# Moving the merge of the dilated branches from VectorE to GpSimd in the blocks of a hybrid attention encoder

## The reference

```python
for window, d in DIL_BRANCHES:              # (128,1), (512,4), (2048,16)
    o, lse = banded_attention(to_sub(q)[:, :, None], to_sub(k), to_sub(v), ...)
w = jax.nn.softmax(jnp.stack(lses), axis=0)
o = jnp.einsum("nbhs,nbhsd->bhsd", w, jnp.stack(outs).astype(jnp.float32))
...
y = jnp.concatenate([rms_norm(merge_heads(oa), ga),
                     rms_norm(merge_heads(ob), gb),
                     rms_norm(merge_heads(oc), gc)], axis=-1)
```

## Time and profile before

| | |
|---|---|
| median of three runs | 2626.75 us (2621.09 to 2628.8) |
| the profiled execution | 2627.53 us, its span 2625.8 us |
| mean granted TensorE clock | 0.977 |
| TensorE busy | 2497.4 us, 95% |
| VectorE busy | 1704.0 us, 65% |
| ScalarE busy | 1061.5 us, 40% |
| GpSimd busy | 515.4 us, 20% |

### The profile page before, as it was taken

The page is one execution under the profiler, slowest core; times in us unless marked ns, Lnnn a source line. Parts: engine busy times, 40 slices in busy tenths (PEclk is TensorE's granted clock), DMA queues, the critical chain, the costliest instruction groups (busy, mean ns, idle before and its releaser), DMA issues. The chain is left out here.

```text
span 2625.8 us, 36088 instructions
## 1 busy us (share of the span) xinstructions
PE 2497.4 (95%) x12576; PEld 2069.1 (79%) x12576; DVE 1704.0 (65%) x3236; ACT 1061.5 (40%) x2072; POOL 515.4 (20%) x414
## 2 busy tenths in 40 slices
PE   6999899989899999999989999999898999999997
PEld 5987787768688888888878878877686888888886
DVE  4288767852755555689844986677447555556896
ACT  3333655543522222344343336555444322223442
POOL 1000210000454544200000003100004444542000
PEclk9999999979999999999989999999799999999999
DMA  5311520022222222541232115100331222226213
GB/s 180 93 48 40 117 70 20 20 98 85 72 81 86 83 71 59 179 151 59 70 127 83 48 37 132 50 20 20 107 108 49 89 80 89 65 65 246 92 52 117
DMA packets 229540, 220.35 MB, mean 84 GB/s; under 512 B 48880, under 2 KB 190576, under 8 KB 229360
## 3 DMA queue, kind: packets, MB, share of 16 engines
q1 hardware_dynamic: 229360, 218.07, 26.3%
HBM read 169.96 MB, written 48.06 MB: 83 GB/s over the span
## 5 line engine op out<-in xcount | busy, mean ns | idle before, releaser
L2131 PE MATMUL psum<-OPH_t,WH 128*128 128x512 f32 x704 | 276.5, 393 | 15.9 <-DVE WL L1643 7.6
L2131 PE MATMUL psum<-OPL_t,WH 128*128 128x512 f32 x704 | 275.4, 391 | 0.0
L2131 PE MATMUL psum<-OPH_t,WL 128*128 128x512 f32 x704 | 275.1, 391 | 0.0
L1643 DVE TENSOR_TENSOR WL<-RAW,WH 128x512 fp32r<-128x512 f32 x132 | 161.8, 1226 | 162.8 <-ACT WH L1149 162.8
L2164 PE MATMUL psum<-ABH 128*128 128x512 f32 x616 | 240.1, 390 | 1.1 <-DVE X L1729 1.1
L2166 PE MATMUL psum<-ABH,ABL 128*128 128x512 f32 x616 | 239.7, 389 | 0.0
L2165 PE MATMUL psum<-ABL,ABH 128*128 128x512 f32 x616 | 239.7, 389 | 0.0
L1016 ACT ACTIVATE T<-T,G 128x192 f32<-128x192 f32 (+3 forms) x352 | 166.0, 472 | 144.4 <-DVE G L1394 141.9
L2131 PE MATMUL psum<-OPH_b,WH 128*128 128x512 f32 x528 | 205.6, 389 | 0.0
L2131 PE MATMUL psum<-OPH_b,WL 128*128 128x512 f32 x528 | 205.4, 389 | 0.0
L2131 PE MATMUL psum<-OPL_b,WH 128*128 128x512 f32 x528 | 205.4, 389 | 0.0
(11 more groups left out here) (214 smaller groups left out, 5417.7 us busy)
## 6 DMA issues: line engine op xcount, KB each, us to landing
RAW<-in_w_gu SPq DMA_DIRECT2D x176, 256.0 KB, 3.8
WDS<-in_w_down SPq DMA_DIRECT2D x88, 256.0 KB, 2.6
UR<-in_w_in SPq DMA_DIRECT2D x56, 256.0 KB, 3.2
g_mid<-GRES SPq DMA_DIRECT2D x28, 512.0 KB, 2.6
WDK<-in_w_down SPq DMA_DIRECT2D x44, 256.0 KB, 6.1
x_res<-X SPq DMA_DIRECT2D x2, 4096.0 KB, 13.5
PR<-in_w_out SPq DMA_DIRECT2D x32, 256.0 KB, 4.5
X<-x_res SPq DMA_DIRECT2D x2, 4096.0 KB, 13.0
```

Of the source, the lines that this page charges most:

```text
L1643: v.tensor_tensor(WL[SLOT[i, j]][:, :, :], w_source(i, j), WH[SLOT[i, j]][:, :, :].bitcast(F32), ALU.subtract).then_inc(w_lo, 1)
L2131: last = t.matmul(dst[:, :], w[SLOT[i, j]][:, k, :], h[o][:, k, :], start=(i in (1, 5, 6) and k == 0 and part == 0), stop=(i in (2, 3, 4) ...
```

## The change

The five operations of the merge (three multiplications by the factors, two additions) are issued by GpSimd, in a function `merge(b)` between the power operation of family b and that of family a, for every block but the last. Each raises a new semaphore `merge_s`; the additions wait for the operation that they build on. VectorE waits for all five in step 9 and takes the reciprocal there. What follows for C moves one step back: YC to step 10, `c_merged` and the squares to 11, the mean to 12, the scaling to 13. A's reciprocal, product, squares and mean and B's scaling keep their steps, A's scaling stays in 9. The tail is a function of its own, `tail_finish`, with the operations and the order of before, on VectorE.

```diff
-            LINKS_OWN, LINKS_LATE = 5, 15
+            LINKS_OWN, LINKS_LATE = 5, 10
...
-                def late_finish(b, s, tail=False):
-                    if s in (0, 1, 2, 3, 4, 5, 6, 7, 8, 9, 10, 11):
+                def late_finish(b, s):
+                    if s < 13:
                         dve.wait_ge(dve_seq, links())
...
                     elif s == 3:
-                        if tail:
-                            dve.wait_ge(tail_squares, 1)
                         mean(1, 384)
+                    elif s == 4:
+                        dve.wait_ge(grp_s, C_GROUPS + 3 * b + 3)
+                        link(v.reciprocal(den[:, 1, 0:4].unsqueeze(2), ga[:, :, HD:V1]))
+                    elif s == 5:
+                        link(v.tensor_tensor(YA.rearrange("p (h d) -> p h d", d=HD), ga[:, :, 0:HD],
+                                             spread(den[:, 1, 0:4], 4), ALU.mult))
+                        scale_y("b", b)
+                    elif s == 6:
+                        squares(0, YA, 256)
+                    elif s == 7:
+                        mean(0, 256)
+                    elif s == 9:
+                        dve.wait_ge(merge_s, 5 * b + 5)
+                        link(v.reciprocal(den[:, 2, :].unsqueeze(2), gc0[:, :, HD:V1]))
+                        scale_y("a", b)
+                    elif s == 10:
+                        link(v.tensor_tensor(YC.rearrange("p (h d) -> p h d", d=HD), gc0[:, :, 0:HD],
+                                             spread(den[:, 2, :], 6), ALU.mult))
+                    elif s == 11:
+                        dve.sem_inc(c_merged, 1)
+                        squares(2, YC, 384)
+                    elif s == 12:
+                        mean(2, 384)
+                    elif s == 13:
+                        scale_y("c", b)
...
+                def merge(b):
+                    pool.wait_ge(c_fac, b + 1)
+                    for i in range(3):
+                        g.tensor_tensor(GC[:, i, 0:6 * V1].rearrange("p (h d) -> p h d", d=V1),
+                                        GC[:, i, 0:6 * V1].rearrange("p (h d) -> p h d", d=V1),
+                                        fac_c[:, i, :].unsqueeze(2).broadcast_to([P, 6, V1]), ALU.mult).then_inc(merge_s, 1)
+                    for i in (1, 2):
+                        pool.wait_ge(merge_s, 5 * b + 2 + i)
+                        g.tensor_tensor(GC[:, 0, 0:6 * V1], GC[:, 0, 0:6 * V1], GC[:, i, 0:6 * V1],
+                                        ALU.add).then_inc(merge_s, 1)
+
                 for b in range(MT):
-                    for fam in (1, 0, 2):
-                        mean_powers(fam, b)
+                    mean_powers(1, b)
+                    if b < MT - 1:
+                        merge(b)
+                    mean_powers(0, b)
+                    mean_powers(2, b)
```

More of the change, by code:

```diff
@@ L350, in build_program @@
             b_shift, b_fac, c_shift, c_fac, c_merged = (sem(n) for n in ("b_shift", "b_fac", "c_shift", "c_fac", "c_merged"))
+            merge_s = sem("merge_s")
             gvar_s, grstd_s, y_s = ([sem(f"{n}_{f}") for f in "abc"] for n in ("gvar_s", "grstd_s", "y_s"))
@@ L1481, in late_finish, with tail_finish @@
                     elif s == 3:
-                        if tail:
-                            dve.wait_ge(tail_squares, 1)
                         mean(1, 384)
+                    elif s == 4:
[23 more added lines that the diff above has]
+                        scale_y("c", b)
+                def tail_finish(b, s):
+                    dve.wait_ge(dve_seq, links())
+                    if s < 2:
+                        late_finish(b, s)
                     elif s in (4, 5):
@@ L1497, in late_finish @@
                                                  spread(den[:, 1, 0:4], 4), ALU.mult))
-                            if not tail:
-                                scale_y("b", b)
+                    elif s == 3:
+                        dve.wait_ge(tail_squares, 1)
+                        mean(1, 384)
                     elif s in (6, 7):
                         link(v.tensor_tensor(GC[:, 0, 0:6 * V1], GC[:, 0, 0:6 * V1], GC[:, s - 5, 0:6 * V1], ALU.add))
[L1502 to L1506, removed]
+                        if s == 7:
+                            dve.wait_ge(tail_squares, 2)
                             mean(0, 256)
@@ L1512, in late_finish @@
                                              spread(den[:, 2, :], 6), ALU.mult))
[L1513 to L1517, removed]
                     elif s == 11:
-                        if tail:
-                            dve.wait_ge(tail_squares, 3)
+                        dve.wait_ge(tail_squares, 3)
                         mean(2, 384)
-                    elif s == 12:
-                        scale_y("c", b)
                 def copy_unit(bd, idx, ev, b_now):
@@ L1602, in _ @@
                 for s in (0, 1, 4, 5, 3, 6, 7, 8, 9):
-                    late_finish(MT - 1, s, tail=True)
+                    tail_finish(MT - 1, s)
                 lo_piece(dve, 16)
                 dve.sem_inc(c_merged, 1)
-                late_finish(MT - 1, 11, tail=True)
+                tail_finish(MT - 1, 11)
                 def lo_mixed(f, part):
```

## The result

The changed kernel takes 2603.89 us, the median of 5 runs (2602.41 to 2605.41), against 2628.8 of the kernel before (5 runs, 2621.09 to 2632.73): a ratio of 0.9908, 95% interval 0.9891 to 0.9925. The profiled execution took 2605.41 us with a span of 2603.7, against 2627.53 and 2625.8 before.

What follows compares the result with a forecast made beforehand. TensorE sets the pace, VectorE's queue limiting half a block. Per block, 1.90 us removed against 2.14 of waits gave, with rounding, +0.23; 14 blocks add 3.2 us to 2626.75: 2630 us (+0.1%), range 2613 to 2642.

Steps and rivals of the forecast that it cites:

- What bounds the kernel: Middle blocks: VectorE's queue limits one half, by little; TensorE idles before tiles 9 and 13, ceiling 1.1 us per block.
- Removed, 1.90 per block ahead of tile 9's minimum: VectorE's queue: three multiplies and one add, 0.475 us each, leave ahead of tile 9's minimum.
- Where to look for collisions: VectorE's A product, scaling of b and squares of A wait for GpSimd's merge: 0.81, 1.00 and 0.33 us.
- I take 1.0: GpSimd's merge: each 128x390 operation takes 1.0 us, from 1.29 scaled by 390/512; bounds 0.83 and 1.29.
- They take turns, one whole operation each: VectorE and GpSimd colliding on SBUF: VectorE gets no two operations in a row while GpSimd waits.
- The sum: Per block 1.90 us removed against waits of 2.14: tile 9's minimum 0.23 later; 14 blocks give +3.2 us.
- That goes whole onto TensorE: The 0.23 us delay of tile 9's minimum passes whole through tile 9's exponential onto TensorE in each block.
- My steps: VectorE's queue timed instruction by instruction among GpSimd's merge operations; tile 9's minimum starts at 49.51 instead of 49.28.
- rival 1: VectorE hardly queues in the blocks because the scaling does not collide: 0.9 us won per block, 2614 us; chance 0.24.
- rival 3: Middle blocks lose TensorE's full clock through more idle time: +35 us, 2662 us; chance 0.10.
- Rival 2: GpSimd's merge ends late, from operations of about 1.03 us on, holding a's scaling: 2634 to 2641 us; chance 0.20.
- Moved at no cost: Later steps of C and the reload released about 1.5 us later were costed at nothing; tile 13 late by 0.23.

Runs made afterwards that it cites:

- wide factors: Changed kernel with the second operand of GpSimd's three multiplications a full-width tile instead of the broadcast factor: 2608.22 us, ratio 0.992.
- one operation late: Changed kernel with one more GpSimd 128x384 addition between family b's power operation and the merge: 2606.05 us, ratio 0.9914.
- three operations late: Changed kernel with three more GpSimd 128x384 additions between family b's power operation and the merge: 2630.29 us, ratio 1.0006.
- the first experiment: Changed kernel with block 6's late finish, which runs inside block 7, back on VectorE in the old steps: 2611.46 us, ratio 0.9943.

## Why the prediction was wrong

- **What bounds the kernel: right for the middle blocks.** TensorE idle ahead of tiles 9 and 13, ceiling 1.1 us per block. The change won 0.87 of it, and 0.27 at tile 13 stays. But the ceiling for the whole, 15 us, multiplied that by 14 as if block 7 were a middle block; the measured 24.9 lies above it.
- **Removed, 1.90 per block ahead of tile 9's minimum: right.** Where to look for collisions: right, in the order given. The scaling, for which no row of before showed a collision, does wait: 0.99 for 0.41, and 1.17 with wide factors. The Trainium skill, "SBUF — State Buffer", section "Who interferes with whom", which says so of tensor_scalar, agrees with this trace.
- **The term "I take 1.0" for GpSimd's operations was mis-sized** for the three that decide. The multiplications take 0.842 (median; 837 the shortest), the additions 1.046. The lower bound, 0.83, was the better guess; widening by 390/512 from a row with two full inputs was not. The Trainium skill, "GPSIMD Engine Reference", section 3.1, with 2.6 cycles an element gave an estimate of 0.85: the multiplications agree with it, the additions don't. With the multiplications at 1.02 the collisions cost 1.57, with 0.84 they cost 1.06 (0.1 of which is TensorE's): 0.51 of the error in the start of tile 9's minimum is this term.
- **"They take turns, one whole operation each" was too dear.** The sum had 2.14 for operations of 1.0; with multiplications of 1.02 the runs show 1.57: 0.57 of the error. The two together, 1.08, are but for rounding the distance from +0.23 to the measured -0.87 in that start. I took from the gate/up stage that GpSimd stands still while VectorE has its turn. In the merge it lost about 0.1 over three operations (0.2 in the version with one operation late).
- **"That goes whole onto TensorE" holds only past a point that I did not look for.** TensorE lets the copy of tile 6 start 2.87 after tile 4's at the earliest, so the first 1.0 of what GpSimd adds ahead of it is hidden. Past that it does pass on: with wide factors the copy came 0.43 later and the period grew by 0.36. My steps had the copy at 3.69, so this did not enter the number, but it took from the chances: any size of collision up to 1.0 gives the same time, and rival 1 should have had more than 0.24. There is a second such point at tile 9: its transposes were held 0.70 with the minimum at 4.81, 0.41 with it at 4.52 (three operations late) and 0.36 with it at 4.47 (wide factors), so they wait for nothing once it starts by 4.11. Of the 0.87 that the minimum came earlier, 0.70 shortened the block. The other 0.17 came from tile 13, where the stall fell from 0.44 to 0.27 and the forecast had it no shorter than before. That the period fell by the same 0.87 as the minimum is a coincidence.
- **The clock of block 7 was left out of the sum.** That is the largest miss: 13.3 of the 24.9 us. I wrote under rival 3 that with rival 1 block 7 "might keep its clock, worth some us per layer", and did not work it out. The earlier trace rows showed that it was there to be won: eight matmuls of 2.17 in block 7, with TensorE idle for 0.95 of 4 us ahead of them, VectorE busy all that time. Their 0.84 is the wrong measure beside it, though, and rival 3 used it: it is another group, in a middle block. The same eight in block 7 take 1.26 with the clock kept (1829.03 in the chain of the changed kernel), so the clock costs it 0.9, and a group of eight for A, 0.84 with the clock kept, takes 1.60 with it lost (1853.86 in the chain before): 0.8, where rival 3 had 1.33, so that its +35 was too much. Rival 1 was therefore priced at 2614; with the 13.3 it would have been about 2601.
- **Rival 1** had the right block (0.9 said, 0.87 measured) for a wrong reason, that the scaling would not collide. **Rival 2** was right as a mechanism: with three operations more it appeared at 2630.29, but it needs far later operations than the 1.03 that I named, since the merge started as forecast and ran 4.86 in place of 6.0. Its wait at step 9 did not show in the changed kernel's middle blocks (in block 7 it is 0.2), where power for family a ended at 1738.98, 1.1 ahead of the scaling of a.
- **Moved at no cost: nearly right.** The product for C in step 10 holds tile 13 by 0.27, not more than before; the reload at step 15 stalls nothing.

The parts add up: 10.4 for twelve middle blocks, 13.3 for the clock and 2.0 for the load in block 7 make 25.7. The medians show 24.9. The spans differ by 22.1 only, since in the profiled execution of the changed kernel the first middle block began 3.4 us later than before (395.25 against 391.84). That start lies anywhere between 391.5 and 395.3 in the twelve traces and is no effect of the change: the changed kernel in its second trace had it at 391.55. Later stages vary too: in this second trace the block begins 3.7 earlier, and its span is only 0.9 shorter. The sum is thus good to a few us.

## What to carry to other kernels

An operation taken off an engine's queue is worth what lies between its old end and the next thing that the queue waits for, and a collision in its place is free up to that same point: work out when the *other* engine would be ready before a wait is passed on in full. Then look at every stretch where the granted clock falls, and at what the change does to the idle time just ahead of it: one block in eight held over half of this gain. A clock that can go either way may also show as a wide spread of single runs (12.6 us in the first experiment, 3.0 in the changed kernel); it is a hint only, since the kernel before, whose trace lost the clock in both layers, spreads by 11.6 too. A few matmuls more are a cheap way to make the loss rarer, but here they didn't rule it out, while every trace with block 7's merge on GpSimd kept the clock, but for the one with three operations put ahead of it.

## What the runs showed of the hardware that I had not expected

- The clock of one place can come out either way with the same code: in one execution it fell in one layer and held in the other after the same 4 us with TensorE busy 3.05, and in another execution so after 3.34; each loss cost 6.0 to 7.3 us. Four more matmuls per layer made the kernel before 13.0 us faster by the medians.
- GpSimd's multiplication by a broadcast factor takes 0.842 us at 128x390, the multiplication by another tile of full width 1.02, the addition of two branches 1.046, and the addition of a tile to itself at 128x384 0.83. So it is not the operation that sets the price, and not the number of inputs alone; what makes a second tile 0.18 dearer stays open.
- VectorE's scaling with one SBUF input and a scalar waited 0.58 for GpSimd, longer than the product with two inputs (0.31), while GpSimd lost about 0.1 to the two together.
